# Moving the transposes of the gated product from TensorE to VectorE in a two-layer decoder trunk

## The reference

```python
def swiglu(x, w_in, w_out):          # w_in 1024 x 5632, w_out 2816 x 1024
    gate, up = jnp.split(x @ w_in, 2, axis=-1)
    return (jax.nn.silu(gate) * up) @ w_out

x = x + 0.5 * swiglu(rmsnorm(x, g), w_in, w_out)
```

## Time and profile before

| | before |
|---|---|
| time, median of 3 runs | 954.72 us (952.33 to 955.31) |
| profiled execution, first to last instruction | 952.5 us |
| TensorE busy | 937.7 us, 98% |
| VectorE busy | 542.6 us, 57% |
| ScalarE busy | 440.6 us, 46% |
| the chain that ended last, TensorE's share | 94% |
| the L1134 transposes of the gated product | 176 matmuls, 26.3 us busy |
| mean granted TensorE clock | 0.997 of full |

### The profile page before, as it was taken

One profiled execution on the slowest core, in us unless ns is written; L12 is line 12 of the kernel. 1 busy time (PEld: TensorE's weight loads), 2 busy tenths in 40 slices (PEclk: granted clock), 3 DMA queues, 4 the chain that ended last, 5 costly groups with the idle time before them and its releaser, 6 DMA issues.

```text
span 952.5 us, 12737 instructions
## 1 busy us (share of the span) xinstructions
PE 937.7 (98%) x4363; PEld 774.3 (81%) x4363; DVE 542.6 (57%) x646; ACT 440.6 (46%) x615; POOL 28.2 (3%) x55
## 2 busy tenths in 40 slices
PE   7999999999999999999999999999999999999997
PEld 6888888888888888888888888888778888888885
DVE  5754554568656545545575454556866574554534
ACT  6553444456435534444354443534565473444432
POOL 1000000000000000000000000000411000000000
PEclk9999999999999999999999999999999999999999
DMA  8756474447644664656456566563440196465631
GB/s 277 255 186 212 147 223 158 155 154 266 221 146 156 189 216 150 213 166 201 145 197 205 180 198 199 162 218 106 156 154 16 48 318 215 151 215 164 199 109 44
DMA packets 122100, 168.81 MB, mean 177 GB/s; under 512 B 8589, under 2 KB 98773, under 8 KB 122069
## 3 DMA queue, kind: packets, MB, share of 16 engines
q1 hardware_dynamic: 121936, 168.35, 54.7%
q10 hardware_dynamic: 132, 0.04, 0.0%
HBM read 167.31 MB, written 1.05 MB: 177 GB/s over the span
## 4 chain that ended last, share of the span: by engine, by line
PE 94%; DVE 1%; DMA 1%; ACT 1%; POOL 1%; issue 1%; SPq 0%; ACTq 0%; DVEq 0%; POOLq 0%
PE acc L1090 30%; PE proj L1074 19%; PE proj L1076 19%; PE proj L1075 19%; PE tp L1134 2%; PE tp L1125 1%; PE tp L1140 1%; DMA raw_in<-in_w_ff_in 1%; PE proj L1272 1%; PE acc L1272 1%; POOL scratch L395 1%; PE acc L1298 1%; PE tp L1298 1%; DVE in_lo L703 0%; ACT gated L457 0%
## 5 line engine op out<-in xcount | busy, mean ns | idle before, releaser
L1074 PE MATMUL proj<-in_hi,xT_hi 128*128 128x512 f32 x848 | 336.9, 397 | 1.0 <-DVE xT_lo L758 0.6
L1076 PE MATMUL proj<-in_hi,xT_lo 128*128 128x512 f32 x848 | 331.4, 391 | 0.0
L1075 PE MATMUL proj<-in_lo,xT_hi 128*128 128x512 f32 x848 | 330.9, 390 | 0.0
L703 DVE TENSOR_TENSOR in_lo<-raw_in,in_hi 128x1024 fp32r<-128x1024 f32 x212 | 251.0, 1224 | 43.5 <-ACT in_hi L420 43.3
L420 ACT ACTIVATE in_hi<-raw_in 128x1024 fp32r<-128x1024 f32 x212 | 212.7, 1051 | 15.7 <-PE proj L1076 6.2
L464 ACT ACTIVATE gated<-proj,rstd 128x256 f32<-128x256 f32 x88 | 41.6, 473 | 363.7 <-PE proj L1076 363.7
L766 DVE SCALAR_TENSOR_TENSOR gated<-proj,rstd,gated 128x256 f32<-128x256 f32 x88 | 42.6, 484 | 274.5 <-ACT gated L464 274.3
L1074 PEld LDWEIGHTS proj<-in_hi,xT_hi 128*128 128x128 f32 x848 | 159.6, 188 | 35.2 <-issue 1.3
L1076 PEld LDWEIGHTS proj<-in_hi,xT_lo 128*128 128x128 f32 x848 | 159.6, 188 | 34.2
L1075 PEld LDWEIGHTS proj<-in_lo,xT_hi 128*128 128x128 f32 x848 | 159.9, 189 | 31.6
L710 DVE TENSOR_TENSOR out_lo<-raw_out,out_hi 128x1024 fp32r<-128x1024 f32 x96 | 114.2, 1230 | 6.1 <-ACT out_hi L428 6.1
(11 more groups left out here) (102 smaller groups left out, 468.4 us busy)
## 6 DMA issues: line engine op xcount, KB each, us to landing
raw_in<-in_w_ff_in SPq DMA_DIRECT2D x352, 256.0 KB
raw_out<-in_w_ff_out SPq DMA_DIRECT2D x88, 512.0 KB, 5.4
raw_in<-in_conv_w_in SPq DMA_DIRECT2D x24, 512.0 KB
raw_in<-in_attn_w_qkv SPq DMA_DIRECT2D x12, 512.0 KB
raw_out<-in_conv_w_out SPq DMA_DIRECT2D x8, 512.0 KB, 5.4
raw_out<-in_attn_w_o SPq DMA_DIRECT2D x8, 512.0 KB, 3.3
x<-in_x SPq DMA_DIRECT2D x2, 512.0 KB, 4.6
scratch<-in_ln_final SPq DMA_DIRECT2D x1, 512.0 KB, 4.2
```

Source lines behind the costliest of these rows:

```text
L703: dve.tensor_tensor(in_lo[:, slot, 2 * q:2 * q + 2, :], raw_in[:, 2 * q:2 * q + 2, :], in_hi[:, slot, 2 * q:2 * q + 2, :].bitcast(F32), AL ...
L1074: pe.matmul(proj[t][:, :], x_hi, in_hi[:, slot, k, :], start=(k == 0), stop=False)
L1075: pe.matmul(proj[t][:, :], x_hi, in_lo[:, slot, k, :], start=False, stop=False)
L1076: last = pe.matmul(proj[t][:, :], x_lo, in_hi[:, slot, k, :], start=False, stop=(k == KD - 1))
```

## The change

In units 0 to 9 of each gated stage VectorE transposes the gated product instead of TensorE. One VectorE transpose turns blocks of 32 x 32; 16 instructions, one for each pair of a source and a target group of 32 partitions, each over 128 elements per partition, move the 256 x 256 tile from hid_buf into a new buffer hT_f in SBUF (a part of scratch that the gated stages don't use). ScalarE and VectorE make the hi and lo parts from hT_f. The new block, move_hidden, stands on VectorE behind unit j's second gated product and the last in piece, ahead of the out tile's lo part; in unit 0 right behind the second gated product. Unit 10 keeps its transposes on TensorE.

```diff
+Q = 32
+        hT_f = scratch[:, 6144:6656].rearrange("p (k n) -> p k n", k=2)
+        hT_moved = sem("hT_moved")
 # ScalarE
-            def hidden_hi(c, slot):
-                act.wait_ge(hT_ps, c + 1)
+            def hidden_hi(f, j, slot):
+                act.wait_ge(hT_moved, (NJ - 1) * f + j + 1)
+                act.activation(hT_hi[:, slot, :, :], hT_f[:, :, :], ACT.Copy).then_inc(hT_hi_done, 1)
+
+            def last_hidden_hi(f, slot):
+                act.wait_ge(hT_ps, f + 1)
...
 # VectorE
-            def hidden(c, t):
+            def hidden(c, t, after=None):
                 dve.wait_ge(silu_done, 2 * c + t + 1)
-                if not isinstance(c, int) or c >= 1:
-                    dve.wait_ge(hT_ps, c)
+                if after is not None:
+                    dve.wait_ge(*after)
...
+            def move_hidden(c):
+
+                dve.wait_ge(h_ready, 2 * c + 2)
+                for b in range(P // Q):
+                    for a in range(P // Q):
+                        last = dve.transpose(
+                            hT_f[a * Q:(a + 1) * Q, :, :].rearrange("p k (t n) -> p k t n", t=NT)[:, :, :, b * Q:(b + 1) * Q],
+                            hid_buf[b * Q:(b + 1) * Q, :, :].rearrange("p t (k n) -> p k t n", k=2)[:, :, :, a * Q:(a + 1) * Q])
+                last.then_inc(hT_moved, 1)
+
             def hidden_lo(c, slot):
+                dve.wait_ge(hT_hi_done, c + 1)
+                dve.tensor_tensor(hT_lo[:, slot, :, :], hT_f[:, :, :],
+                                  hT_hi[:, slot, :, :].bitcast(F32), ALU.subtract).then_inc(hT_lo_done, 1)
...
-                    hidden(c, 0)
+                    hidden(c, 0, (hT_ps, f) if f else None)
                     split_in(u + 1, (u + 1) % 2, (2, 3))
                     hidden(c, 1)
+                    move_hidden(c)
                     split_out(o, o % 2)
                     if s == 0:
                         rope_angles()
                     def middle(j, par):
-                        hidden(c + j, 0)
+                        hidden(c + j, 0, (hT_moved, (NJ - 1) * f + j))
                         hidden_lo(c + j - 1, (c + par + 1) % 2)
                         split_in(u + j + 1, (u + par + 1) % 2, (0, 1, 2))
                         hidden(c + j, 1)
                         split_in(u + j + 1, (u + par + 1) % 2, (3,))
+                        move_hidden(c + j)
                         split_out(o + j, (o + par) % 2)
...
 # TensorE
             def transpose_hidden(c):
                 pe.wait_ge(h_ready, 2 * c + 2)
-                if not isinstance(c, int) or c >= 1:
-                    pe.wait_ge(hT_lo_done, c)
...
                             project(m, u + j, t, (u + par) % 2, fresh=(start and t == 0))
-                            if t == 0:
-                                transpose_hidden(c + j - 1)
...
                         project(m, u + j, t, (u + j) % 2)
-                        if t == 0:
-                            transpose_hidden(c + j - 1)
```

More of the change, by code:

```diff
@@ L489, in _ @@
                 if kind == FF:
-                    c = NJ * FF_INDEX[s]
+                    f, c = FF_INDEX[s], NJ * FF_INDEX[s]
                     if s > 0 and STAGES[s - 1] != FF:
@@ L504, in middle @@
                         silu(c + j, u + j, 0)
-                        hidden_hi(c + j - 1, (c + par + 1) % 2)
+                        hidden_hi(f, j - 1, (c + par + 1) % 2)
                         split_in(u + j + 1, (u + par + 1) % 2, (0, 1, 2))
@@ L516, in _ @@
                     silu(c + j, u + j, 0)
-                    hidden_hi(c + j - 1, (c + j - 1) % 2)
+                    hidden_hi(f, j - 1, (c + j - 1) % 2)
                     split_out(o + j, (o + j) % 2)
@@ L521, in _ @@
                     silu(c + j, u + j, 1)
-                    hidden_hi(c + j, (c + j) % 2)
+                    last_hidden_hi(f, (c + j) % 2)
                     if next_u:
@@ L768, in hidden, with last_hidden_lo @@
                                          op0=ALU.mult, op1=ALU.mult).then_inc(h_ready, 1)
+            def move_hidden(c):
[6 more added lines that the diff above has]
+                last.then_inc(hT_moved, 1)
             def hidden_lo(c, slot):
+                dve.wait_ge(hT_hi_done, c + 1)
+                dve.tensor_tensor(hT_lo[:, slot, :, :], hT_f[:, :, :],
+                                  hT_hi[:, slot, :, :].bitcast(F32), ALU.subtract).then_inc(hT_lo_done, 1)
+            def last_hidden_lo(c, slot):
                 dve.wait_ge(hT_hi_done, c + 1)
@@ L841, in _ @@
                     hidden(c + j, 1)
-                    hidden_lo(c + j, (c + j) % 2)
+                    last_hidden_lo(c + j, (c + j) % 2)
                     if next_u:
```

## The result

The changed kernel takes **943.83 us** (median of four runs, 941.38 to 944.04) against 955.01 us for the kernel before (four runs, 952.33 to 956.13). The ratio is 0.9877, with a 95% interval of 0.9861 to 0.9893: 1.2% faster. The forecast was 942.4 us. The profiled execution took 943.97 us, of which its span is 942.1 us; the span before was 952.5 us, so 10.4 us came off where the sum had said 12.35. The four runs of the changed kernel spanned 939.5 to 942.1 us, so the profiled one is among the longest; the medians lie 11.2 us apart.

The account below looks back on a forecast made before the run. TensorE, 94% of the chain, was taken as the bound. -19.2 + 4.4 (stage 0) + 1.7 (clock) + 0.75 (stage 5) = -12.35 us gave span 940.2, time 942.4 us, 1.3% faster; the forecast's own range was 940 to 944.5.

Parts of the forecast that it names:

- The removal: Units 0 to 9 of four gated stages lose their TensorE transposes: 40 x 0.48 = 19.2 us off.
- The block: M, sixteen VectorE transposes per unit: 5.2 us at pitch 0.325, the serial case (no overlap); range 1.8 to 7.2.
- In a steady unit it hides: Steady gated unit: M fits VectorE's idle piece of 6.43 us, VectorE busy 13.85 in 16.32, no cost.
- Start of stage 0: TensorE stalls 4.4 us for the lo part of unit 0's gated product after unit 1's projections.
- The clock behind it: After stage 0's stall the granted clock falls to half, costing 1.7 us (0 to 3.4).
- Start of stage 5: TensorE stalls 0.75 us in unit 1 for the lo part of unit 0's gated product.
- Stages 2 and 3: Starts of these stages: lo part ready before TensorE needs it, no stall up to M = 6.2.
- Unit 10: Last out tile's load, issued M later, lands after L (3.3 us): M + L is 8.5, under 9.4, no stall.
- rival 1: Late last out tile in unit 10: L of 5.4, stalls add 3.8 us, time 946.2; chance 0.12.
- cheap and the half-rate transposes: VectorE transposes, cheap: M 3.3 or 1.8, time 936.5 to 940, chance 0.13; half rate: M 7.2, time 952, chance 0.08.
- Nothing comes off: Rival: TensorE's transposes were already hidden, so removing them takes nothing off TensorE; chance under 1%.
- VectorE as the bound: Rival: above a pitch of 0.46 us VectorE limits the gated unit; 980 us at 0.50; chance 0.11.

Follow-up runs that it names:

- removal_alone: Changed kernel with each unit's sixteen VectorE transposes replaced by one over 128 partitions x 512 elements (product not the reference's): 934.72 us, ratio 0.9790 to the kernel before.
- same_partitions: Changed kernel with each VectorE transpose writing to the 32 partitions it reads (product not the reference's): 940.72 us in one run.
- angles_later: Changed kernel with the rotary angles and the two sines moved from unit 0 to behind unit 1 of stage 0: 938.13 us, ratio 0.9815 to the kernel before.
- out_tile_first: Changed kernel with the out tile's lo part ahead of the VectorE transposes in units 1 to 9: 942.24 us, ratio 0.9863 to the kernel before.
- angles_and_out: Changed kernel with the edits of angles_later and out_tile_first together: 937.47 us, ratio 0.9812 to the kernel before.
- moves_24: Changed kernel with eight further VectorE transposes in each unit's block, written to SBUF nobody reads: 964.38 us, ratio 1.0088 to the kernel before.
- gpsimd_alone: Changed kernel with VectorE, in attention, waiting for GpSimd's rotated keys before unit 2's in tile lo parts: 943.53 us, ratio 0.9868 to the kernel before.
- moves_32: Changed kernel with sixteen further VectorE transposes in each unit's block, written to SBUF nobody reads: 1060.68 us in one run.
- filled_stall: Changed kernel with 38 unused identity transposes on TensorE just ahead of the wait that stalls it in stage 0: 941.98 us, ratio 0.9866 to the kernel before.

## Why the prediction came out right, point by point

**The removal** (-19.2): right, to the hundredth in the steady unit, 16.32 us; removal_alone gave 20.8 in the span, of which 1.6 are a fall of the clock in attention that it didn't have.

**The block** (M = 5.2): 5.05 measured. The 0.29 us per instruction was 0.302, the gap of 0.035 was 0.014, the pitch 0.316 for 0.325. That the serial case was the one to take is shown by same_partitions: with the partitions kept the pitch is 0.197. The prediction's rows alone didn't decide it; being nearer in size was a weak reason. The rule of the Trainium skill, VectorE: DVE Perf Modes, section "Two Vector instructions with no wait between them", that an instruction with its output in another quadrant of partitions is held until the earlier ones have finished, agrees with these two numbers. The Trainium skill's preference on the same page, in "Rules for kernel authors", for TensorE doesn't fit this kernel: TensorE is the bound and VectorE idles, and the change by itself is 1.2% faster.

**In a steady unit it hides** (0): right. 13.50 us of VectorE where 13.85 was said, 1.36 us of idle left where 1.2 was.

**Start of stage 0** (+4.4): right, 4.40, and angles_later shows what made it that long.

**The clock behind it** (+1.7): the mechanism right, the size off: 2.5, of which 2.1 is the clock and the rest the slower restart. The figure was copied from a wait of 2.2 us. Behind the longer one the clock had fallen before TensorE restarted, so a half-speed stretch of 4.6 us fell on matmuls. And the short wait was a poor model in another way: in attention TensorE waited 2.2 to 3.3 us for GpSimd in eleven of the traces, and the clock fell behind it in six (2.2 us in the kernel before, 3.2 in the changed one, angles_later, out_tile_first, angles_and_out and same_partitions) and stayed at 1.00 in five (2.2 us in removal_alone and moves_24, 2.7 in gpsimd_alone, 3.2 in moves_32, 3.3 in filled_stall). That the price came near was in part luck in the row that was at hand. What decides whether the clock falls behind such a wait, these runs don't show. At the start of stage 0 it fell in every trace with an idle wait of 2.9 to 9.5 us, six in all. The changed kernel's time also varied: the four runs of the changed kernel had spans of 939.5 to 942.1 us at mean clocks of 0.996 to 0.992, the longer ones at the lower clock. That falls of the clock make the spread was not tried.

**Start of stage 5** (+0.75): +0.4 of wait and +0.3 of slower matmuls behind it, of which an earlier landing of the in tile hid 0.45. The size was right, the split not. This wait is in no way firm: angles_later, out_tile_first and gpsimd_alone, whose edits don't shorten stage 5's start, have none there. What moved it is open; the landing of the in tile is a candidate.

**Stages 2 and 3** (0): right, no wait of TensorE there at their starts.

**Unit 10** (0, since L = 3.3): this is the step that was mis-sized. L was 4.34 us, between the two values that I had weighed, and M + L = 5.05 + 4.34 = 9.4, on the threshold itself: the gated product ended at 189.51 (189.03 and 0.48), with the transposes due at 189.33. It cost +1.1 in place of 0 (rival 1 at 5.4 would have been +3.8), in stages 0 and 2 about half of it in waits of 0.23 us and half in the slower transposes behind them, for which the sum had no term. out_tile_first took it away. Why a load takes 4.3 us there, and not 3.3, stays open.

**Left out: attention** (0 in the sum): +1.0. No instruction of attention was changed, but VectorE's in pieces came to lie beside all of GpSimd's rotations of the keys instead of a part of them: before, the last of these ran in 0.45 us. That those pieces are what slows GpSimd is shown by gpsimd_alone; what spared the last rotation before is a pause of VectorE, which waited 0.50 us for ScalarE's hi part ahead of the fourth piece; in the changed kernel the four run in a row. From the kernel before:

```profile
683.11 0.45 POOL L396 TENSOR_TENSOR scratch<-gated 128x128 f32<-128x128 f32 x1
683.33 1.31 DVE L703 TENSOR_TENSOR in_lo<-raw_in,in_hi 128x1024 fp32r<-128x1024 f32 x1 [0.50 <-ACT in_hi L420]
```

removal_alone (0.65 us) and moves_24 (1.10 us) have this pause, and their wait is the old 2.2 us, though moves_24 has the longer block. So the 1.0 us is no fixed price of the block. Why ScalarE's hi part came in time in one kernel and not in the other is only argued, from when the transfers landed.

**The rivals.** The cheap and the half-rate transposes were settled by the duration, 302 ns. "Nothing comes off" by 16.32. VectorE as the bound was not reached; moves_32 shows that it exists, at a block of some 8 us and not 7.4.

The errors: 0.8 for the clock, 1.1 for unit 10 and 1.0 for attention, less 0.5 at stage 5 and 0.5 of small ones, make the 1.9 us between the forecast span of 940.2 and 942.1. The first two lay within the bounds that the prediction had given; the third had no term. They partly cancel, and the shortest of the four runs spanned 939.5 us, under the forecast; so the mechanism is confirmed row by row, and that the total came within 2 us owes something to luck.

## What to carry to other kernels

Work moved from the bound engine to an idle one costs nothing in the steady loop as long as it fits the idle piece there, and is paid at the edges, where that engine has other work in a row: here 19.2 us came off in 40 units and 9 us went back in six places, and moving a few calls and adding two waits won nearly all of that back. Price a stall with the clock that may fall behind it, take that price from waits of the same length, and look at more than one: behind the short ones here it fell in about half of the traces. When a step has a threshold, as M + L > 9.4, and the candidate values lie on its two sides, put a part of the cost into the sum instead of none.

## What the runs showed of the hardware

- A VectorE transpose of 32 x 128 fp32 takes 302 ns when each writes another group of 32 partitions than the one ahead, and 256 to 260 ns when it stays in the group; the pitches are 0.316 and 0.197 us. With the change of group go both the overlap and some 45 ns of duration. One of 128 x 512 takes 705 ns, close to a tensor_tensor of that size (690 ns).
- GpSimd's tensor_tensor of 128x128 fp32 took 0.46 us alone and 1.43 us beside VectorE's in_lo; that of 128x256 0.74 and 1.63 to 1.70 us beside its out_lo. Two- to threefold was more than I had looked for, and it decides a wait of TensorE.
- TensorE's clock went to the 1.2 GHz level within a wait of 4.4 us. Behind waits of 2.2 to 3.3 us in attention it did so in six traces of eleven (2.2 us and half clock in the kernel before, 2.2 us and full clock in removal_alone), and not behind 0.5 us in angles_later. With transposes in the wait of stage 0 (filled_stall, one trace) it stayed at 2.4 GHz.
